# Expert features in order 8p+k: wider runs for the up weights, and rows turned by VectorE instead of TensorE

## The chip, the core and the metric

The kernel runs on one core of a Trainium2 chip. The metric is the device time of one execution in microseconds (us), as the median of several runs. The profiled execution is a separate one.

## What is computed

One layer of a hybrid backbone, for 512 sample tokens and 128 prompt tokens of 1024 features, all in fp32. A first part (modulated norm, one input projection, gated linear attention beside spatial gating, an output projection) is followed by a mixture of 16 experts in which each expert chooses its tokens. The second part, in which most of the time lies, is this:

```python
def ec_moe(x, router_w, w1, w3, w2):
    probs = jax.nn.softmax(jnp.matmul(xf, router_w), axis=-1)
    cap = EC_CAPACITY_FACTOR * N // N_EXPERTS            # 64 sample rows, 16 prompt rows
    gates, idx = lax.top_k(probs.T, cap)
    xe = xf[idx]
    h = jax.nn.silu(jnp.einsum('ecd,edf->ecf', xe, w1)) * jnp.einsum('ecd,edf->ecf', xe, w3)
    ye = jnp.einsum('ecf,efd->ecd', h, w2) * gates[..., None]
    out = jnp.zeros_like(xf).at[idx.reshape(-1)].add(ye.reshape(-1, D))
# in trunk_layer
    h2 = rmsnorm(x, norm2_w) * (1.0 + scale2) + shift2
    x = x + gate2 * ec_moe(h2, router_w, w1, w3, w2)
```

The weights w1 and w3 are 1024 x 2048 for each expert and w2 is 2048 x 1024: 24 MB an expert, 403 MB in all.

## The kernel before

Every engine runs its own list of instructions, written by hand, and semaphores join them. SyncE issues the loads of weights, ScalarE does activations and copies, VectorE the elementwise work and the 32x32 block transposes, GpSimd the loads and saves that are looked up by a table, TensorE the products and the turns of 128x128 tiles.

**Ahead of the experts.** The modulation vectors (shift, scale, gate, twice) come out of TensorE as rows in 12 pieces of 512 (`ada_product`), ScalarE copies them to `ada_rows`, TensorE turns them (`ada_turn`, L651 to L654, four turns each) and VectorE stores them in `mod` with the bias added (`store_mod`, L1391, L1393). Pieces 6 to 9 are shift 2 and scale 2, those of the mixture's norm. Feature f lies on partition f mod 128, in column f div 128 (order 128k+p). The normed rows `xn2` are turned by `route_turn` (L890), 8 tiles of 128 columns for each token tile, and multiplied with the router's weights. GpSimd saves each tile of `xn2` to DRAM (L585). VectorE finds the top tokens; the tables of slots are turned by TensorE (`all_slots`, L995).

**An expert.** TensorE holds 96 slots of rows (64 sample, 16 prompt, 16 empty) in three parts of 32 as `xe`, turned to [128 partitions, 8 kt, slots], and streams the weights past them (`up`, L1016, four products side by side in the array's four column groups). Weights come in 12 chunks of 2 MB an expert: 8 up chunks, w1 and w3 in turns, of two kt each, and 4 down chunks. They go through a ring of six slots; SyncE issues the next load of a slot when TensorE has read it (`load_expert_chunk`, L522). An up chunk is read by rows k*128+p, so that each partition's part is two runs of 8 KB; a down chunk is read by rows 16p+f, one run of 16 KB for each partition and 64 KB from partition to partition. The last up chunks of w1 and of w3 are done part by part, so that ScalarE (`silu`, L1321) and VectorE can start on part 0: the product with the gate (L1745) and the transpose of 32x32 blocks to `h` (L1749), which counts up `h_turned[part]`. The down products (`down_sample` L1032, `down_prompt` L1043) wait for `h_turned[0]` and `[1]`, and from the first `down_prompt` on for `[2]`.

**The next expert's rows.** GpSimd gathers 80 rows of 4 KB from the saved `xn2` to `xe_rows` (L588), TensorE turns them in eight tiles after the up products (`turn_xe`, L967), and VectorE multiplies by `amp2` and adds `mod`'s shift on the way to `xe` (`modulate`, L1662, L1667). GpSimd issues the gather for the expert after that when the turns are done. At the end of an expert VectorE scales the results (L1763, L1768, L1776) and GpSimd adds them to the rows in DRAM (scatter-add, L615). TensorE waits at the end of an expert for `xe` to be complete:

```python
                if not last:
                    pe.wait_ge(gathered, 32 + expert * 16)
                    for half in range(2):
                        wait_role_free(pe, f"X_{half}", expert)
                        role_filled(turn_xe(role_bank(f"X_{half}"), half), f"X_{half}")
                wait_role_free(pe, "Y_A", expert)
                wait_role_free(pe, "Y_B", expert)
                for part in range(PARTS - 1):
                    pe.wait_ge(h_turned[part], expert + 1)
```

## Time and profile before

| | us |
|---|---|
| median of 3 runs | 1450.53 (1450.44 to 1455.31) |
| the profiled execution | 1455.17 |
| its span | 1453.3 |
| TensorE busy (products) | 1391.0, 96% |
| VectorE busy | 356.9, 25% |
| ScalarE busy | 163.7, 11% |
| GpSimd busy | 56.0, 4% |
| bytes moved | 469.56 MB, mean 323 GB/s |

PE is TensorE's products, PEld its weight loads, DVE is VectorE, ACT ScalarE, POOL GpSimd, SPq SyncE's sequencer. L12 is line 12 of the kernel. Queue q1 is SyncE's, q10 ScalarE's and q0 GpSimd's. An fp32 product shows as two instructions, a turn as one. A row of the timeline or of the chain merges like instructions that follow one another. In the page's second part each digit or number is one of 40 equal slices of the span, here 36.3 us each.

### The profile page before, as it was taken

What the parts mean: (1) busy time and instruction counts of PE and PEld (TensorE: products, weight loads), DVE (VectorE), ACT (ScalarE), POOL (GpSimd) and SP (SyncE); (2) the same over time, 40 slices, a digit from 0 to 9 for tenths busy, and PEclk for the clock granted to TensorE, in tenths of its full rate; (3) what the DMA queues carried; (4) which work ended last, traced back from release to release, by engine and by line L of the source; (5) the groups of instructions that cost most, each with busy time, mean ns of one, the idle gap of its engine ahead of it and who ended that gap; (6) DMA issues with size and microseconds to landing.
All of it is one profiled execution on the core that took longest, in us unless ns stands there. A gap on an engine that the chain in (4) does not pass through costs nothing.

```text
span 1453.3 us, 24452 instructions
## 1 busy us (share of the span) xinstructions
PE 1391.0 (96%) x10960; PEld 511.1 (35%) x10960; DVE 356.9 (25%) x709; ACT 163.7 (11%) x263; POOL 56.0 (4%) x65
## 2 busy tenths in 40 slices
PE   5899999899879999999999999999999999999994
PEld 2354544755533232323333333332323333232321
DVE  3116153523632111303111130211203111130314
ACT  3263324111120000000000000000000000000011
POOL 0200000000000000000000000000000000000000
PEclk8999999799989999999999999999999999999997
DMA  9433313401656999999999999999999999999995
GB/s 358 160 118 115 107 51 109 154 30 58 263 222 279 396 409 413 411 417 400 426 402 412 414 412 417 401 412 414 410 417 402 425 399 412 414 410 417 414 411 213
DMA packets 73357, 469.56 MB, mean 323 GB/s; under 512 B 4749, under 2 KB 6626, under 8 KB 32362
## 3 DMA queue, kind: packets, MB, share of 16 engines
q1 hardware_dynamic: 67200, 451.36, 76.3%
q0 software_dynamic: 5200, 17.17, 4.2%
q10 hardware_dynamic: 922, 0.52, 0.1%
q8 instruction: 27, 0.44, 0.1%
q14 instruction: 8, 0.07, 0.0%
HBM read 455.67 MB, written 13.37 MB: 323 GB/s over the span
## 4 chain that ended last, share of the span: by engine, by line
PE 85%; DMA 11%; DVE 2%; issue 1%; SPq 1%; ACT 1%; POOLq 0%; ACTq 0%; POOL 0%; DVEq 0%
PE psum L1016 41%; PE psum L1032 12%; PE psum L663 9%; DMA ring<-in_exp_w_dram 9%; PE psum L1043 6%; PE psum L876 5%; PE psum L707 2%; PE psum L644 1%; DMA ring<-in_ada_w_dram 1%; PE psum L967 1%; PE psum L901 1%; PE psum L850 1%; SPq L546 1%; PE psum L854 1%; DMA both<-xn_dram,both 1%
## 5 line engine op out<-in xcount | busy, mean ns | idle before, releaser
L1016 PE MATMUL psum<-ring,both 128*32 128x512 f32 x6144 | 665.4, 593 | 1.9 <-DMA ring<-in_exp_w_dram 0.8
L1016 PEld LDWEIGHTS psum<-ring,both 128*32 128x32 f32 x6144 | 198.0, 110 | 462.7 <-issue 434.7
L1032 PE MATMUL psum<-ring,both 128*32 128x512 f32 x2048 | 233.6, 597 | 6.3 <-DMA ring<-in_exp_w_dram 5.8
L1745 DVE TENSOR_TENSOR both<-both,psum 128x512 f32<-128x512 f32 x48 | 49.5, 1032 | 555.4 <-PE psum L1016 555.4
L663 PE MATMUL psum<-ring,feat 128*128 128x512 f32 x320 | 138.3, 593 | 0.0
L1321 ACT ACTIVATE both<-psum 128x512 f32<-128x512 f32 x48 | 28.7, 597 | 952.1 <-PE psum L1016 887.1
L1032 PEld LDWEIGHTS psum<-ring,both 128*32 128x32 f32 x2048 | 65.2, 110 | 154.0 <-issue 143.8
L1043 PE MATMUL psum<-ring,both 128*32 128x512 f32 x1024 | 118.7, 592 | 0.0
L663 PEld LDWEIGHTS psum<-ring,feat 128*128 128x128 f32 x320 | 60.5, 190 | 76.4 <-issue 76.3
L1763 DVE SCALAR_TENSOR_TENSOR both<-psum,both 64x512 f32<-64x512 f32 x32 | 24.0, 749 | 224.2 <-PE psum L1043 224.0
L876 PE MATMUL psum<-ring,both 128*128 128x512 f32 x160 | 73.9, 618 | 0.0
L1043 PEld LDWEIGHTS psum<-ring,both 128*32 128x32 f32 x1024 | 33.4, 110 | 76.5 <-issue 75.9
L876 PEld LDWEIGHTS psum<-ring,both 128*128 128x128 f32 x160 | 31.1, 200 | 36.5 <-issue 36.4
L707 PE MATMUL psum<-feat,ring 128*128 128x512 f32 x64 | 32.0, 656 | 4.0 <-ACT feat L1152 2.4
L615 POOL DMA_INDIRECT acc_dram<-both x15 | 21.6, 1441 | 355.6 <-DVE both L1776 355.6
L588 POOL DMA_INDIRECT both<-xn_dram,both x15 | 13.8, 917 | 541.9 <-PE psum L967 541.6
L1749 DVE STREAM_TRANSPOSE both<-both 128x512 f32<-128x512 f32 x48 | 34.1, 711 | 1.7
L644 PE MATMUL psum<-ring,silu_c 128*32 128x512 f32 x192 | 26.3, 675 | 3.7 <-DMA ring<-in_ada_w_dram 3.1
L1776 DVE SCALAR_TENSOR_TENSOR both<-psum,both 64x512 f32<-64x512 f32 x32 | 24.0, 750 | 6.8 <-PE psum L1032 6.6
L1768 DVE TENSOR_TENSOR both<-both 32x512 f32<-32x512 f32 x32 | 21.9, 683 | 0.8
L1483 DVE SCALAR_TENSOR_TENSOR both<-both,chunk_decay 64x128 f32<-64x128 f32 x64 | 18.3, 347 | 14.7 <-ACT both L1225 14.3
L707 PEld LDWEIGHTS psum<-feat,ring 128*128 128x128 f32 x64 | 12.9, 208 | 21.2 <-issue 21.2
(221 smaller groups left out, 604.6 us busy)
## 6 DMA issues: line engine op xcount, KB each, us to landing
ring<-in_exp_w_dram SPq DMA_DIRECT2D x192, 2048.0 KB, 25.0
ring<-in_ada_w_dram SPq DMA_DIRECT2D x12, 2048.0 KB, 12.5
ring<-in_w_in_dram SPq DMA_DIRECT2D x4, 2048.0 KB, 12.8
ring<-in_w_out_dram SPq DMA_DIRECT2D x2, 2048.0 KB, 10.6
acc_dram<-x POOLq DMA_DIRECT2D x5, 512.0 KB, 2.9
xn_dram<-feat POOLq DMA_DIRECT2D x5, 512.0 KB, 2.9
x<-acc_dram SPq DMA_DIRECT2D x5, 512.0 KB, 26.5
out_dram<-feat SPq DMA_DIRECT2D x5, 512.0 KB, 10.4
```

The source lines that it names most:

```text
L644: mm = nc.tensor.matmul(bank(n)[gr * PART:(gr + 1) * PART, :], silu_c[:, kt, :], w[:, kt, :], start=(i == 0), stop=(i == 1))
L663: mm = nc.tensor.matmul(bank(n), hT[:, kt, t * P:(t + 1) * P], w[:, kt, :], start=(kt == 0), stop=(kt == KT - 1))
L707: return nc.tensor.matmul(bank(JOB["qkS", m]), w[:, kt, m * P:(m + 1) * P], hT[:, kt, 0:SAMPLE], start=(kt == 0), stop=(kt == KT - 1))
L876: mm = nc.tensor.matmul(bank(n), mixT[:, t % 2, kt, :], w[:, kt, :], start=(kt == 0), stop=(kt == KT - 1))
L1016: mm = nc.tensor.matmul(role_bank(role)[f4 * PART:(f4 + 1) * PART, :], xe[:, kt, part * PART:(part + 1) * PART], w[:, kt % 2, f4 * 512:(f4 ...
L1032: mm = nc.tensor.matmul(role_bank("Y_A")[at:at + PART, :], h[:, c, part * PART:(part + 1) * PART], w[:, f, half * 512:(half + 1) * 512], s ...
L1043: mm = nc.tensor.matmul(role_bank("Y_B")[at:at + PART, :], h[:, c, 2 * PART:PADDED], w[:, f + odd, half * 512:(half + 1) * 512], start=(c ...
L1321: role_stored(nc.scalar.activation(silu_h[:, r % 2, :], role_bank(role), ACT.Silu), role)
L1745: role_stored(nc.vector.tensor_tensor(h_rows[:, part, :].rearrange("p (c a) -> p a c", a=PART), silu_h[:, part % 2, :].rearrange("p (a c) ...
L1749: nc.vector.transpose(h[:, :, part * PART:(part + 1) * PART], h_rows[:, part, :].rearrange("p (c a) -> p c a", a=PART))\
L1763: ins = nc.vector.scalar_tensor_tensor(y_pair[:, odd, :], y_b[rows], prob_now[rows, 1:2], gate2_p[rows], ALU.mult, ALU.mult)
L1776: ins = nc.vector.scalar_tensor_tensor(y[0:CAP_S, cols], y_a[rows], prob_now[rows, 0:1], gate2_s[rows], ALU.mult, ALU.mult)
```

## The change

The features of the mixture's input are held in order 8p+k (feature 8p+k on partition p, column k) instead of 128k+p. For this:

- an up chunk is read by rows 8p+k, two neighbouring rows at a time: one run of 16 KB for each partition, 64 KB from partition to partition; the router's weights are read in the same order;
- norm2's weights and the biases of shift 2 and scale 2 are loaded in this order by three small DMAs of GpSimd (`vecs2`); pieces 6 to 9 of the modulation are turned by `ada_turn_by_row`, eight products of 64 stepped columns of `ada_rows` against `sel` (128 x 2, which sums the row groups), and stored by `store_mod_by_row`;
- `route_turn` and the turns of the first expert's rows take every eighth column (`by_row`);
- a gather fetches each row in four quarters of 1 KB, quarter a of slot s to partition 32a+s, in three DMAs of 128 quarters (`xq`), with three more tables of indices (`slot_quarter`), worked out by five small VectorE operations and turned by three more of TensorE;
- VectorE transposes the 32x32 blocks of `xq` straight to `xe` (three instructions of 128x256) and applies amplitude and shift in four operations on whole slot ranges; this stands where `modulate` stood, after the transposes of `h`;
- TensorE's eight turns per expert, its waits for them and their PSUM roles go; TensorE waits for `xe_ready` at the head of experts 1 to 15; GpSimd issues the three gathers for the expert after next when VectorE has turned `xq`.

```diff
@@ load_expert_chunk
-                    src = (w1, w3)[which][0, bass.ds(expert, 1)].rearrange("a (k p) n -> p (a k) n", p=P)[:, 2 * k2:2 * k2 + 2, :]
+                    src = (w1, w3)[which][0, bass.ds(expert, 1)].rearrange("a (p k) n -> p (a k) n", p=P)[:, 2 * k2:2 * k2 + 2, :]
@@ gpsimd
-            pool.dma_start(router, router_w[0].rearrange("(k p) e -> p k e", p=P)).then_inc(router_loaded, 16)
+            pool.dma_start(router, router_w[0].rearrange("(p k) e -> p k e", k=KT)).then_inc(router_loaded, 16)
+            for i, src in enumerate((norm2_w[0], ada_b[0, 128 * SHIFT2:128 * SHIFT2 + D], ada_b[0, 128 * SCALE2:128 * SCALE2 + D])):
+                pool.dma_start(vecs2[:, i, :], src.rearrange("(p k) -> p k", k=KT)).then_inc(vecs2_loaded, 16)
             def gather(expert):
-                pool.indirect_dma_start(out=xe_rows, out_offset=None, in_=xn2_dram,
-                                        in_offset=bass.IndirectOffsetOnAxis(ap=slot_tok[0:SLOTS, expert:expert + 1], axis=0))\
-                    .then_inc(gathered, 16)
+                for part in range(PARTS):
+                    pool.indirect_dma_start(out=xq[:, part, :], out_offset=None, in_=xn2_dram.rearrange("t (a n) -> (t a) n", a=4),
+                                            in_offset=bass.IndirectOffsetOnAxis(ap=slot_quarter[:, part, expert:expert + 1], axis=0))\
+                        .then_inc(gathered, 16)
...
-                    wait_role_filled(pool, "X_0", expert)
-                    wait_role_filled(pool, "X_1", expert)
+                    pool.wait_ge(xq_turned, expert + 1)
                     gather(expert + 2)
@@ tensor
+            def ada_turn_by_row(c5):
+                wait_stored(pe, JOB["adaR", c5])
+                pe.wait_ge(sel_ready, 1)
+                n = JOB["adaT", c5]
+                wait_bank_free(pe, n)
+                rows = ada_rows[:, ADA_ORDER.index(c5) % 2, :].rearrange("p (m k) -> p k m", k=KT)
+                at = (c5 % 2) * (P // 2)
+                for k8 in range(KT):
+                    mm = nc.tensor.matmul(bank(n)[at:at + P // 2, 2 * k8:2 * k8 + 2], rows[:, k8, :], sel, start=True, stop=True)
+                filled(mm, n)
...
+            def by_row(rows):
+                return rows.rearrange("p (m k) -> p k m", k=KT)
...
-                        mm = nc.tensor.transpose(bank(n)[:, j * P:(j + 1) * P], xn2[:, t, kt * P:(kt + 1) * P], ident)
+                        mm = nc.tensor.transpose(bank(n)[:, j * P:(j + 1) * P], by_row(xn2[:, t, :])[:, kt, :], ident)
...
-                for i in range(5):
+                for i in range(8):
                     mm = nc.tensor.transpose(bank(n)[:, i * EXPERTS:(i + 1) * EXPERTS], top_rows[:, i, :], ident[0:EXPERTS, 0:EXPERTS])
...
+                if not first:
+                    pe.wait_ge(xe_ready, expert)
...
-                if not last:
-                    pe.wait_ge(gathered, 32 + expert * 16)
-                    for half in range(2):
-                        wait_role_free(pe, f"X_{half}", expert)
-                        role_filled(turn_xe(role_bank(f"X_{half}"), half), f"X_{half}")
...
-                if not last:
-                    for half in range(2):
-                        wait_role_stored(pe, f"X_{half}", expert)
@@ vector, expert_work
-                    for half in range(2):
-                        wait_role_filled(dve, f"X_{half}", expert)
-                        role_stored(modulate(role_bank(f"X_{half}"), half, link_expert), f"X_{half}")
+                    dve.wait_ge(gathered, 16 + 48 + expert * 48)
+                    for part in range(PARTS):
+                        ins = nc.vector.transpose(xe[:, :, part * PART:(part + 1) * PART], xq[:, part, :].rearrange("p (i k) -> p k i", k=KT))
+                    ins.then_inc(xq_turned, 1)
+                    dve.wait_ge(xq_turned, expert + 1)
+                    kinds = ((slice(0, CAP_S), 0), (slice(CAP_S, PADDED), 1))
+                    for slots, w in kinds:
+                        shape = [P, KT, slots.stop - slots.start]
+                        ins = nc.vector.tensor_tensor(xe[:, :, slots], xe[:, :, slots], amp2[:, :, w:w + 1].to_broadcast(shape), ALU.mult)
+                    link_expert(ins)
+                    for slots, w in kinds:
+                        shape = [P, KT, slots.stop - slots.start]
+                        ins = nc.vector.tensor_tensor(xe[:, :, slots], xe[:, :, slots], mod[:, SHIFT2:SHIFT2 + KT, w:w + 1].to_broadcast(shape),
+                                                      ALU.add)
+                    ins.then_inc(xe_ready, 1)
```

## Rows read from the trace of the kernel before

**Rows 1.** The page: engine TensorE, and the rate of the 40 slices.

```profile
PE 1391.0 (96%) x10960; PEld 511.1 (35%) x10960; DVE 356.9 (25%) x709; ACT 163.7 (11%) x263; POOL 56.0 (4%) x65
...
GB/s 358 160 118 115 107 51 109 154 30 58 263 222 279 396 409 413 411 417 400 426 402 412 414 412 417 401 412 414 410 417 402 425 399 412 414 410 417 414 411 213
```

**Rows 2.** Busy time in 14 periods, one for each of experts 1 to 14.

```profile
core 0: us, PE busy (x) PEld busy (x) DVE busy (x) ACT busy (x) POOL busy (x), PEclk, DMA share, GB/s
489.80:552.90 63.10, 62.76 (x588) 19.05 (x584) 11.60 (x22) 1.79 (x3) 2.42 (x2) 1.00 1.01 409
...
678.80:741.40 62.60, 62.60 (x588) 19.21 (x584) 11.63 (x21) 1.79 (x3) 2.35 (x2) 1.00 1.01 412
...
sum 879.30, PE 878.38 PEld 268.07 DVE 162.69 ACT 25.08 POOL 32.11; mean PE 62.74 PEld 19.15 DVE 11.62 ACT 1.79 POOL 2.29
```

**Rows 3.** The chain that ended last, 660 to 760 us: start, us, what.

```profile
678.76 41.20 PE psum L1016 x384
719.96 0.70 PE psum L967 x8
720.67 3.57 PE psum L1032 x32
```

**Rows 4.** SyncE's loads L522 issued in 741 to 804 us: issue to landing.

```profile
DMA to landing us min/median/max: 23.7/24.8/25.1
```

**Rows 5.** DMA queues (packets, MB, share) in 714-724, 736-746 and 752-762 us.

```profile
q1 hardware_dynamic: 293, 4.28, 100.4%
...
q1 hardware_dynamic: 545, 4.20, 100.9%
...
q1 hardware_dynamic: 554, 4.28, 101.1%
```

**Rows 6.** DMA queues in 726-731 us (a gather) and 748-752 us (a scatter-add).

```profile
q1 hardware_dynamic: 97, 1.39, 84.5%
q0 software_dynamic: 82, 0.29, 17.4%
...
q1 hardware_dynamic: 138, 1.06, 64.3%
q0 software_dynamic: 94, 0.32, 40.1%
```

**Rows 7.** DMA queues in 44-47 us (512 B beside 2 KB) and 26-29 us.

```profile
q1 hardware_dynamic: 427, 0.87, 80.3%
q10 hardware_dynamic: 426, 0.22, 25.8%
...
q1 hardware_dynamic: 569, 1.16, 105.0%
```

**Rows 8.** Timeline, DVE 714 to 745 us, then PE 700 to 860 us.

```profile
718.40 1.01 DVE L1745 TENSOR_TENSOR both<-both,psum 128x512 f32<-128x512 f32 x1
719.44 0.71 DVE L1749 STREAM_TRANSPOSE both<-both 128x512 f32<-128x512 f32 x1
...
721.13 0.71 DVE L1749 STREAM_TRANSPOSE both<-both 128x512 f32<-128x512 f32 x1
...
738.11 1.51 DVE L1763 SCALAR_TENSOR_TENSOR both<-psum,both 64x512 f32<-64x512 f32 x2 [14.17 <-PE psum L1043]
...
719.90 0.77 PE L967 MATMUL psum<-consts,both 80*128 80x80 f32 x8
720.60 3.64 PE L1032 MATMUL psum<-ring,both 128*32 128x512 f32 x32
```

**Rows 9.** Timeline of PE and DVE ahead of the experts' loop.

```profile
212.85 0.60 PE L653 MATMUL psum<-consts,both 128*128 128x128 f32 x4
...
424.32 1.96 PE L901 MATMUL psum<-router_amp,both 128*128 128x16 f32 x16
...
408.24 0.67 DVE L1557 TENSOR_TENSOR both<-psum,both 128x512 f32<-128x512 f32 x1
...
417.95 0.42 DVE L1662 TENSOR_TENSOR both<-psum,amp 128x256 f32<-128x256 f32 x1 [1.31 <-PE psum L976]
```

## What is predicted, and why

> **What bounds the kernel now.** I read the page first: TensorE is busy for 96% of the span, and from slice 14 on the core moves 396 to 426 GB/s in every slice [rows 1]. So the page leaves two candidates for the sixteen experts, which fill everything behind 420 us. The table by expert then gives the period. From the first up product of expert 1 (489.8 us) to that of expert 15 (1369.1 us) pass 879.3 us, 62.80 us for each of 14 experts, with the DMA share at 1.01 and the clock at full in each of them [rows 2]. The first period is 63.10 us, the fourth 62.60.
>
> TensorE's own part of a period comes from the chain: 41.20 us of up products, 0.70 us of turns of the next expert's rows, 3.57 us for the first group of down products [rows 3], and five more groups of 3.43 us worth of products; eight up chunks and four down chunks are 12 times 5.15 = 61.8 us, and with the turns 62.5 us. The queue's own part comes from the issues: in the period from 741 us on a 2 MB load lands 23.7 to 25.1 us after its issue [rows 4]. At the 5.0 us that one load takes (next paragraph), that is five loads waiting or moving, out of six slots, so the queue is nearly never empty. Both servers thus need 62.5 to 62.8 us, and whichever edit helps only one of them is worth little. That is the main thing to see.
>
> **Up weights in 16 KB runs.** I priced them from stretches in which only SyncE's queue moved. The semaphore writes (32 in 10 us) are taken off the count. Of the down weights, which already come in 16 KB runs with 64 KB from run to run, 261 packets took 100.4% of 16 engines for 10 us: 160.6/261 = 0.615 us each. Of the up weights' 8 KB packets there are two levels: 513 packets at 100.9% make 0.315 us, 522 at 101.1% make 0.310 us; mean 0.3125 [rows 5]. A chunk costs each engine 16 x 0.3125 = 5.00 us now and 8 x 0.615 = 4.92 us then. The new up pattern (16 KB runs, 64 KB apart) is just that of the down weights, so I take their price. Saved: 0.08 us a chunk (0.04 to 0.12 by the two levels), 0.64 us an expert. The queue's period goes from 62.80 to 62.16 us if the gather costs what it did.
>
> **The gather as quarters.** Today 80 packets of 4 KB are fetched while 16 KB packets run. In 726 to 731 us 1.68 MB moved, which at the 428 GB/s of the neighbouring stretch takes 3.93 us; 1.07 us are lost beside the 0.77 us of the gather's own 0.33 MB: 1.84 us a gather, 0.37 us for each of an engine's 5 packets [rows 6]. The scatter-add, same count at 748 to 752 us, costs about 1.5 us in the same way, and stays [rows 6]. The new gather moves 384 packets of 1 KB, 24 an engine. No 1 KB packets beside a busy queue are in the trace. The nearest rows are the 512 B packets beside 2 KB ones at 44 to 47 us: 418 of them take 25.8% of 3 us, 0.030 us each, while the 2 KB packets beside them stay at 0.090 us, against 0.089 us with nothing beside them [rows 7]. By a line through 512 B (0.030) and 2 KB (0.089) a 1 KB packet is 0.05 us, 24 of them 1.2 us: 0.6 us less than now. The other end is the present price per packet, 24 x 0.37 = 8.8 us: 7 us more. In between, the present price by bytes: 1.84 x 0.393/0.328 = 2.2 us, 0.4 us more. I take the middle of the first and the third, 1.7 us, because the packets nearest in size slow nobody and the packets nearest in path (same queue, same table) slow others; that is about no change. The queue's period is then 62.1 us (61.5 to 62.6, and up to 69 in the rival below).
>
> **No turns on TensorE.** The eight turns go, 0.70 us each time, 15 times: 10.5 us of TensorE's time. But they cover something. The first down product waits for h of parts 0 and 1. VectorE finishes the product of part 1 at 719.41 and its transpose at 720.15; TensorE's up products end at 719.9, so the turns up to 720.60 hide that wait [rows 8]. With them gone TensorE stands still from 719.9 to about 720.2. The saving is 720.6 - 720.2 = 0.4 us an expert, not 0.7. h of part 2 is there at 721.84 and needed 3.4 us into the down products: no wait. TensorE's period becomes 62.5 - 0.4 = 62.1 us.
>
> **What VectorE takes over.** Behind the last h transpose (721.84) come three transposes of 128x256 and four elementwise operations. The transpose of 128x512 takes 0.71 us [rows 8], so 0.36 us each. An operation that writes at a step (the h product, 1.01 us) is 1.5 times one of the same shape that doesn't (0.67 us) [rows 8, 9], so with the stepped reads up to 0.55 us each. Elementwise: two of 512 columns (0.7) and two of 256 (0.42). In all 3.3 to 3.9 us, done by 725.8. VectorE's next job starts at 738.11 [rows 8], and TensorE's new wait for xe comes at 741: hidden with 12 us to spare. If a gather landed more than 40 us late this wait would show; it has a whole period. Queued behind VectorE's new wait for the gather are the y products, needed from 738 on. GpSimd's three gathers per expert are issued at about 723; even at one 1 KB packet for each 16 KB packet they are through after 24 x 0.665 = 16 us, ahead of the scatter-add, which is queued behind them and starts at about 743.
>
> **Ahead of the experts.** Turns of shift and scale 6 to 9 become eight matmuls against two columns. Four turn instructions take 0.60 us; small matmuls run in pairs of passes, 16 in 1.96 us, 0.12 us each [rows 9], so 16 instructions cost up to 2.0 us, or 1.3 if two columns are a third cheaper. Turns 6 and 7 stand on TensorE's chain: +0.7 to +1.4 us each. Turns 8 and 9 come before TensorE waits for VectorE: nothing. Reads at a 32 B step in the token turns, three more small transposes, three tiny loads on GpSimd's queue, five small VectorE operations more for the slot table: covered by waits of TensorE for VectorE or DMA, 0 to +2 us. I take +2 in all (0 to +5).
>
> **The sum.** The larger of 62.1 and 62.1 us, with a little for two servers that are equal (today 62.80 against 62.5 and 62.8): 62.3 us. 14 x (62.80 - 62.3) = 7.0 us, and for the turns of expert 0 and the up chunks of expert 15 0.8 us. Less 2 us ahead: 5.8 us. The profiled execution took 1455.2 us (span 1453.3) and would take 1449.4; it stands 4.6 us above the median of the runs, 1450.5. Against the median: **1444.7 us**, own range 1442 to 1449. A measurement of this kernel can tell about 0.5% (7.25 us) from no change, so faster means under 1443.3, slower over 1457.8.
>
> **Rivals.**
> A. *The gather becomes cheap and the start costs nothing.* For it: the 512 B packets of [rows 7]. Against it: equal servers never reach their floor. Period 62.2, 14 x 0.6 + 0.8 = 9.2 us, less 0 to 1: 1441.8. Chance 0.27. The swizzle rule above would lead here.
> B. *The gather takes back what the runs give.* It costs 2.5 us, 0.7 more than now; period 62.8, only the start moves: 1449 to 1453. Chance 0.15. An up weight's 16 KB run that is no faster than its two halves ends here as well.
> C. *Small packets are paid by the piece (slower).* Place: the queue, 727 to 745 us of each period. Above 0.105 us a packet (24 x 0.105 = 2.5 us) the gather eats the gain; at half of today's price per piece, 0.185 us, it costs 4.4 us, 2.6 more than now, period 64.8, 14 x 2.0 + 2 = 30 us: 1480. For it: 4 KB gather packets cost 0.37 us where 0.154 us would be their bytes. Chance 0.12.
> D. *The start costs more,* because weights are loaded at a 32 B step in some 60 turns: 0.1 to 0.2 us each, 6 to 12 us, with the gain of the experts at half: 1450 to 1459. Chance 0.08, half of it over 1457.8. The Trainium skill, "SBUF — State Buffer", section "Door 1: The DMA port swizzle", says that reads which leave a 16-byte line each time pay a penalty; the trace agrees for VectorE's writes (1.01 against 0.67 us) and shows nothing of TensorE.
>
> The forecast has 0.38. **Chances:** faster 0.27 + 0.08 of the forecast's range = 0.35; slower 0.12 + 0.04 and 0.02 for a stall not thought of = 0.18; same 0.47. The range takes in A, the forecast, B and D: 1439.5 to 1460.
>
> **What would show it.** Right: SyncE's packets of 16 KB at 0.615 us throughout; a period of 62.3 us; the first down product 0.3 us behind the last up product, released by VectorE's transpose; the next expert's xe ready at 726. Wrong: 16 KB packets of the up weights above 0.63 us; a gather stretch of more than 2.5 us lost; TensorE waiting at the head of an expert for VectorE; a first up product of expert 1 that is late by more than the 2 us.

## The result, and the profile after

The changed kernel takes 1439.53 us (median of 5 runs, 1436.43 to 1440.22), the kernel before 1450.44 us (5 runs, 1448.50 to 1455.31): a ratio of 0.992, 95% interval 0.990 to 0.994, 10.9 us faster. The forecast was 5.8 us faster. Later runs of the changed kernel on another chip gave 1442.38 us beside 1451.82 us for the kernel before, 9.4 us faster.

The page of the profiled execution (its time 1439.8 us). The lines answer to [rows 1]; behind them are the page's lines on queues and issues.

```profile
span 1438.0 us, 24229 instructions
PE 1378.7 (96%) x10891; PEld 565.4 (39%) x10891; DVE 383.0 (27%) x704; ACT 163.1 (11%) x263; POOL 93.3 (6%) x98
GB/s 357 162 125 101 98 49 111 183 30 59 245 245 259 416 426 419 427 421 416 430 417 427 420 427 421 417 430 416 426 422 426 419 416 430 418 427 419 404 406 123
q0 software_dynamic: 6016, 18.17, 4.2%
ring<-in_exp_w_dram SPq DMA_DIRECT2D x192, 2048.0 KB, 17.4
x<-acc_dram SPq DMA_DIRECT2D x5, 512.0 KB, 14.8
```

A weight load now lands 17.4 us after its issue in the median; before it was 25.0. A load is issued when its slot of the ring has been read, and its chunk is needed five chunks later, by my estimate after 5 x 5.15 = 25.8 us. What is left between landing and need I call the queue's lead: before it was under 2 us in the loop's middle, and in the changed kernel it grows from expert to expert. The landing of the loads issued in 1300 to 1355 us (least, median, most), first before, then changed:

```profile
DMA to landing us min/median/max: 21.9/23.7/24.9
```

```profile
DMA to landing us min/median/max: 8.9/10.2/11.3
```

Earlier in the changed kernel the median was 23.1 us (issued in 560 to 620 us) and 20.0 us (741 to 804 us, against the 24.8 of [rows 4]). Next the stretches: 14 periods (from the first up product of expert 1 to that of expert 15), and the last expert up to the first of the two save instructions that GpSimd issues last. First the changed kernel, then the kernel before, whose 14 periods are those of [rows 2] to within 0.3 us.

```profile
core 0: us, PE busy (x) PEld busy (x) DVE busy (x) ACT busy (x) POOL busy (x), PEclk, DMA share, GB/s
485.20:1357.80 872.60, 868.05 (x8068) 315.46 (x8064) 186.34 (x280) 25.07 (x42) 63.85 (x53) 1.00 1.01 422
1357.80:1428.30 70.50, 62.25 (x580) 22.39 (x572) 21.94 (x29) 10.96 (x21) 2.41 (x3) 0.98 0.77 308
```

```profile
489.30:1368.90 879.60, 878.68 (x8184) 268.16 (x8180) 162.93 (x294) 25.08 (x42) 32.11 (x27) 1.00 1.01 412
1368.90:1446.20 77.30, 64.28 (x580) 18.90 (x572) 21.90 (x29) 11.43 (x21) 2.36 (x2) 0.95 0.86 348
```

The periods are 872.6/14 = 62.33 us each, with no scatter beyond 0.01 us: 7.0 us less in all. The last expert takes 70.5 instead of 77.3 us: 6.9 us less. Where those went shows in the waits of TensorE (engine, line, waited for: us in total, times, longest) in the last expert of the kernel before:

```profile
PE psum L1032 <- DMA ring<-in_exp_w_dram: 4.6, 1, 4.6
PE psum L1032 <- DVE both L1749: 0.5, 1, 0.5
```

In the changed kernel only the second kind is left there. Behind the wait of 4.6 us TensorE also works at a lower clock. The first row is its group of down products behind the wait, which takes 5.34 us where the same group takes 3.65 us in the changed kernel; the other two are 1421.2 to 1423 and 1423 to 1425 us, with a granted clock of 0.58 and 0.52, so mostly at the lower of the two levels (1.2 GHz of 2.4):

```profile
1421.21 5.34 PE L1032 MATMUL psum<-ring,both 128*32 128x512 f32 x32 [4.64 <-DMA ring<-in_exp_w_dram]
1421.20:1423.00 1.80, 1.79 (x12) 0.59 (x16) 1.80 (x3) 0.00 (x0) 0.00 (x0) 0.58 1.03 437
1423.00:1425.00 2.00, 2.00 (x12) 0.44 (x8) 2.00 (x2) 0.00 (x0) 0.00 (x0) 0.52 1.00 426
```

So the 6.9 us are some 4.8 us of waiting, 1.7 us of slower products behind it, and 0.4 us up to the first down product, of which 0.2 us are a wait for weights. The chain of one period of the changed kernel answers to [rows 3]:

```profile
672.38 41.20 PE psum L1035 x384
713.58 0.33 issue
713.90 3.64 PE psum L1051 x32
717.54 1.72 PE psum L1062 x16
719.26 3.43 PE psum L1051 x32
```

The 0.70 us of turns are gone, a pause of 0.33 us stands in their place, and the first group of down products takes 3.64 instead of 3.57 us. VectorE's timeline of the same place (to be held against [rows 8]) gives the cause of the pause: the second h transpose ends at 713.80 (713.09 + 0.71), and the down products start at 713.90.

```profile
713.09 0.71 DVE L1795 STREAM_TRANSPOSE both<-both 128x512 f32<-128x512 f32 x1
713.73 1.03 DVE L1791 TENSOR_TENSOR both<-both,psum 128x512 f32<-128x512 f32 x1
714.79 0.71 DVE L1795 STREAM_TRANSPOSE both<-both 128x512 f32<-128x512 f32 x1
715.42 1.67 DVE L1802 STREAM_TRANSPOSE both<-both 128x256 f32<-128x256 f32 x3
717.12 1.03 DVE L1808 TENSOR_TENSOR both<-both,amp 128x512 f32<-128x512 f32 x2
718.18 1.03 DVE L1812 TENSOR_TENSOR both<-both,mod 128x512 f32<-128x512 f32 x2
731.41 1.51 DVE L1821 SCALAR_TENSOR_TENSOR both<-psum,both 64x512 f32<-64x512 f32 x2 [12.19 <-PE psum L1062]
```

### The profile page after: what moved, and what is told of

Same layout as the page of the kernel before. It is cut to its first block, busy times and chain, and to the rows that moved or that the text cites. A ratio compares the mean times of both kernels' runs of the same rounds, so it can differ in the third digit from the quotient of the medians.

```text
span 1438.0 us, 24229 instructions
## 1 busy us (share of the span) xinstructions
PE 1378.7 (96%) x10891; PEld 565.4 (39%) x10891; DVE 383.0 (27%) x704; ACT 163.1 (11%) x263; POOL 93.3 (6%) x98
## 4 chain that ended last, share of the span: by engine, by line
PE 93%; DVE 3%; DMA 2%; issue 1%; ACT 1%; POOLq 0%; ACTq 0%; POOL 0%; DVEq 0%
PE psum L1035 45%; PE psum L1051 15%; PE psum L685 10%; PE psum L1062 8%; PE psum L898 5%; PE psum L729 2%; PE psum L654 1%; DMA both<-xn_dram,both 1%; PE psum L927 1%; DMA ring<-in_ada_w_dram 1%; PE psum L872 1%; PE psum L876 1%; PE psum L760 0%; PE psum L699 0%; DMA ring<-in_pos_col_dram 0%
## 5 line engine op out<-in xcount | busy, mean ns | idle before, releaser
L1035 PEld LDWEIGHTS psum<-ring,both 128*32 128x32 f32 x6144 | 238.7, 110 | 419.4 <-issue 416.1
L685 PE MATMUL psum<-ring,feat 128*128 128x512 f32 x320 | 138.3, 593 | 0.0
L1051 PEld LDWEIGHTS psum<-ring,both 128*32 128x32 f32 x2048 | 78.5, 110 | 150.1 <-issue 150.1
L685 PEld LDWEIGHTS psum<-ring,feat 128*128 128x128 f32 x320 | 60.5, 190 | 76.4 <-issue 76.3
L600 POOL DMA_INDIRECT both<-xn_dram,both x45 | 49.4, 1099 | 578.5 <-DVE both L1802 569.1
L1062 PEld LDWEIGHTS psum<-ring,both 128*32 128x32 f32 x1024 | 40.3, 110 | 69.6 <-issue 69.3
L625 POOL DMA_INDIRECT acc_dram<-both x15 | 22.1, 1471 | 274.7 <-DVE both L1834 274.7
L1802 DVE STREAM_TRANSPOSE both<-both 128x256 f32<-128x256 f32 x45 | 25.1, 609 | 0.0
## 6 DMA issues: line engine op xcount, KB each, us to landing
ring<-in_exp_w_dram SPq DMA_DIRECT2D x192, 2048.0 KB, 17.4
```

Source lines behind the costliest of these rows:

```text
L600: pool.indirect_dma_start(out=xq[:, part, :], out_offset=None, in_=xn2_dram.rearrange("t (a n) -> (t a) n", a=4), in_offset=bass.IndirectO ...
L685: mm = nc.tensor.matmul(bank(n), hT[:, kt, t * P:(t + 1) * P], w[:, kt, :], start=(kt == 0), stop=(kt == KT - 1))
L1035: mm = nc.tensor.matmul(role_bank(role)[f4 * PART:(f4 + 1) * PART, :], xe[:, kt, part * PART:(part + 1) * PART], w[:, kt % 2, f4 * 512:(f4 ...
L1051: mm = nc.tensor.matmul(role_bank("Y_A")[at:at + PART, :], h[:, c, part * PART:(part + 1) * PART], w[:, f, half * 512:(half + 1) * 512], s ...
L1062: mm = nc.tensor.matmul(role_bank("Y_B")[at:at + PART, :], h[:, c, 2 * PART:PADDED], w[:, f + odd, half * 512:(half + 1) * 512], start=(c ...
L1802: ins = nc.vector.transpose(xe[:, :, part * PART:(part + 1) * PART], xq[:, part, :].rearrange("p (i k) -> p k i", k=KT))
```

## The experiments

In the table the start is where the first up product of expert 1 begins, the loop the mean of 14 periods, the last expert runs from its first up product to the first of the last two saves, and the end from there to the end of the span. They are read from the timelines of TensorE and GpSimd in each kernel's one profiled execution. The median is that of the runs.

| kernel | start | period | last expert | end | median us |
|---|---|---|---|---|---|
| before | 489.3 | 62.83 | 77.4 | 7.0 | 1450.44 |
| before again | 483.3 | 62.89 | 77.7 | 7.0 | 1449.48 |
| changed | 485.2 | 62.33 | 70.4 | 9.7 | 1439.53 |
| changed again | 486.4 | 62.33 | 70.4 | 9.7 | 1442.38 |
| before, 16 KB runs | 485.8 | 62.64 | 70.4 | 7.0 | 1440.32 |
| changed, 8 KB runs | 482.0 | 62.37 | 70.5 | 9.7 | 1440.61 |
| changed, row gather | 487.4 | 62.41 | 73.0 | 7.3 | 1444.96 |
| changed, 8 KB runs and row gather | 488.6 | 62.85 | 77.5 | 7.3 | 1452.49 |
| changed, turns back | 487.2 | 62.64 | 70.4 | 9.7 | 1444.85 |
| before, small reload | 489.1 | 62.85 | 70.8 | 7.0 | 1444.91 |
| changed, part 2 last | 482.5 | 61.80 | 69.7 | 9.7 | 1433.73 |
| changed, part 2 last, again | 487.6 | 61.80 | 69.7 | 9.7 | 1433.74 |
| changed, old turns at the start | 481.7 | 62.33 | 70.4 | 9.7 | 1441.98 |
| before, filler | 488.6 | 62.76 | 77.9 | 7.1 | 1454.46 |

The times of single runs of one kernel scatter by some us either way. The periods and the last expert's time scatter far less: two executions of the changed kernel agree to 0.01 us in the period and 0.1 us in the last expert, two of the kernel before to 0.06 and 0.3 us. So the verdicts rest on these two columns.

**Runs alone.** The kernel before, with the up chunks read by rows 8p+k; the products pair other features, the work is the same.

```diff
-                    src = (w1, w3)[which][0, bass.ds(expert, 1)].rearrange("a (k p) n -> p (a k) n", p=P)[:, 2 * k2:2 * k2 + 2, :]
+                    src = (w1, w3)[which][0, bass.ds(expert, 1)].rearrange("a (p k) n -> p (a k) n", p=P)[:, 2 * k2:2 * k2 + 2, :]
```

> The kernel before with one edit: up chunks are read by rows 8p+k, so in 16 KB runs, while xe keeps its old order (the products mix other features; the work is the same). Theory 1, two equal servers: the queue loses 0.6 us of work an expert, TensorE's 62.5 us stay; the period falls from 62.80 to 62.6 us, 3 us over the loop, and as the queue gains a small lead, part of the 5.8 us that TensorE waits for it at the end of expert 15 goes: 1444 to 1448 us in all, 2 to 6 us less than before. Theory 2, TensorE was the bound all along and the turns are the whole gain: nothing, 1449 to 1451 us. Theory 3, the queue was the bound: 62.2 us and 8 us or more less, 1442 us or below.

Measured: 1440.32 us (4 runs, 1438.73 to 1442.05), beside 1451.87 us for the kernel before on the same chip, ratio 0.993 (0.990 to 0.995). Its two stretches:

```profile
485.80:1362.80 877.00, 877.00 (x8184) 269.11 (x8180) 162.81 (x294) 25.09 (x42) 32.10 (x27) 1.00 1.01 416
1362.80:1433.10 70.30, 62.16 (x580) 19.63 (x572) 21.90 (x29) 10.87 (x21) 2.36 (x2) 0.97 0.86 348
```

The period is 62.64 us, which is TensorE's floor with turns: in these 14 periods it is never idle, and a load lands after 22.1 us in the median instead of 25.0 (18.8 us in 1300 to 1355 us). The loop gives 2.6 us, as theory 1 has it, but the last expert gives the whole 7 us, more than theory 1 had. The total is that of theory 3, whose period of 62.2 us did not come. This one edit reaches the time of the whole change.

**The changed kernel without the runs.** The same line the other way round.

> The changed kernel with up chunks read by rows 128k+p again, in 8 KB runs (the products mix other features). Theory 1: the queue then needs 8 x 5.00 + 4 x 4.92 = 59.7 us for the weights, 1.0 for the cheap gather and 1.7 for the scatter-add, 62.4 us against TensorE's 62.33: period 62.4 to 62.5, landing back from 17 to about 25 us, and part of the wait at the end returns; 1441 to 1445 us against 1439.5. Theory 2: no difference, 1439 to 1440.

Measured: 1440.61 us (4 runs, 1437.23 to 1442.44), ratio 0.994 (0.991 to 0.996). Period 62.84 us once, then 62.33; last expert 70.5 us. Theory 2 holds: the period is TensorE's, not the 62.4 to 62.5 us of theory 1, and no wait comes back at the end. With the cheap gather the queue stays below TensorE's 62.33 us even in 8 KB runs. What it loses is lead: landing 21.7 instead of 17.4 us in the median (17.9 against 10.2 us in 1300 to 1355 us).

**The changed kernel with the old gather.** Experts 1 to 15 then work on rows that the gather doesn't fill.

```diff
             def gather(expert):
-                for part in range(PARTS):
-                    pool.indirect_dma_start(out=xq[:, part, :], out_offset=None, in_=xn2_dram.rearrange("t (a n) -> (t a) n", a=4),
-                                            in_offset=bass.IndirectOffsetOnAxis(ap=slot_quarter[:, part, expert:expert + 1], axis=0))\
-                        .then_inc(gathered, 16)
+                pool.indirect_dma_start(out=xe_rows, out_offset=None, in_=xn2_dram,
+                                        in_offset=bass.IndirectOffsetOnAxis(ap=slot_tok[0:SLOTS, expert:expert + 1], axis=0))\
+                    .then_inc(gathered, 16)
...
-                    dve.wait_ge(gathered, 16 + 48 + expert * 48)
+                    dve.wait_ge(gathered, 16 + 16 + expert * 16)
```

> The changed kernel with the old gather: one DMA of 80 rows of 4 KB to 80 partitions instead of three of 128 quarters; VectorE transposes the same amount, from memory that the gather doesn't fill (the experts 1 to 15 work on other numbers). Theory 1 (the gather to 128 partitions became cheap, 1.0 us of the queue instead of 1.8): the queue needs 59.1 + 1.8 + 1.7 = 62.6 us, period 62.6 against 62.33, 4 us over the loop and 2 to 4 us at the end: 1443 to 1448 us. Theory 2: no difference, 1439 to 1440. In the trace the 16 KB packets beside the gather go from 0.636 back to about 0.83 us under theory 1.

Measured: 1444.96 us (10 runs, 1436.05 to 1451.07), ratio 0.996 (0.993 to 0.998). Against theory 1 the period stays at 62.33 us after the first; the last expert takes 73.0 us, 2.6 more than in the changed kernel, with a wait of 2.4 us for weights. So the median lies in theory 1's range, but not for its reason: the 59.1 + 1.8 + 1.7 = 62.6 us that I added up for the queue are some 0.3 us too much. The gather's own price is close to the expected one: (5 - 1.73 MB/429) + 0.32/429 = 1.7 us, and 0.77 instead of 0.83 us for a 16 KB packet beside it. The queues while a gather runs (packets, MB, share of 16 engines), first this kernel in 725 to 730 us, then the changed kernel in 722 to 728 us:

```profile
DMA packets 195, 1.73 MB, mean 347 GB/s; under 512 B 30, under 2 KB 30, under 8 KB 109
q1 hardware_dynamic: 101, 1.41, 82.8%
q0 software_dynamic: 94, 0.32, 19.2%
```

```profile
DMA packets 290, 2.55 MB, mean 425 GB/s; under 512 B 66, under 2 KB 66, under 8 KB 157
q1 hardware_dynamic: 151, 2.18, 88.0%
```

The row gather pulls the rate down to 347 GB/s, as in [rows 6]. Beside the quarters it is 425 GB/s, against 429 in an undisturbed stretch (736 to 741 us). So a gather of quarters costs its bytes, 0.393 MB/429 = 0.92 us, and next to nothing more: 2.55 MB/429 is 5.94 of the 6 us. The two gathers differ in the size of their pieces, in the number of their DMAs and in the number of partitions; no run tells these apart.

**Both helps to the queue taken away.** The two edits above together; what is left of the change is TensorE without turns, and the start.

> The changed kernel with both helps to the queue taken away: up chunks in 8 KB runs and the old gather of 80 rows (the products mix other features, and VectorE transposes memory that the gather doesn't fill). What is left of the change is TensorE without turns, and the start. Theory 1 (equal servers): TensorE's floor is 62.33 us but the queue needs as long as before, so the period stays at 62.7 to 62.8 us and the last expert, from its first up product to the last save, takes 77 us as before instead of 70.4: 1448 to 1451 us, nearly the whole gain gone. Theory 2 (the turns are the gain): 62.33 and 70.4 us, 1440 us.

Measured: 1452.49 us (10 runs, 1445.91 to 1455.59), ratio 1.000 (0.998 to 1.002). Its two stretches:

```profile
488.60:1368.40 879.80, 870.94 (x8068) 285.32 (x8064) 186.16 (x280) 25.10 (x42) 36.44 (x27) 1.00 1.01 412
1368.40:1446.00 77.60, 64.29 (x580) 19.80 (x572) 21.90 (x29) 11.52 (x21) 2.41 (x3) 0.95 0.86 349
```

They are the stretches of the kernel before, to 0.3 us. Taking the turns from TensorE is worth nothing by itself: over the 14 periods it is busy for 7.7 us less and idle for 8.0 us more (8.9 against 0.9 us). Of these 8.9 us the pauses for h are at most 14 x 0.33 = 4.6 us, the rest is waiting for weights. Its weight loads show the same: 53.2 us in 93 waits for the queue, against 35.9 us in 62 before.

**Turns back on TensorE.** The changed kernel with eight turns of a constant behind the up products.

```diff
+                if not last:
+                    wait_role_stored(pe, "R1_0", expert)
+                    for j in range(8):
+                        nc.tensor.transpose(role_bank("R1_0")[:, (j % 4) * SLOTS:(j % 4 + 1) * SLOTS], ident[0:SLOTS, :], ident[0:SLOTS, 0:SLOTS])
                 wait_role_free(pe, "Y_A", expert)
```

> The changed kernel with eight turns of 80x128 on TensorE put back behind the up products (they turn a constant; nobody reads them). If the turns cover the wait for h, as the prediction said: the 0.33 us of waiting go and 0.70 us of turns come, period 62.33 + 0.4 = 62.7 us, 15 x 0.4 = 6 us more, 1445 to 1446 us. If the wait were not covered by them, 15 x 0.7 = 10.5 us more, 1450 us.

Measured: 1444.85 us (10 runs, 1440.20 to 1449.06), ratio 0.995 (0.993 to 0.997). All 14 periods are 62.64 us: 0.31 us more than 62.33, 14 x 0.31 = 4.3 us; the last expert, which has no turns, is level (70.4 us). The turns did cover the wait for h; without them TensorE gets 0.31 us, not 0.70 (and not the 0.4 of the prediction).

**The reload in the last expert.** The kernel before, with 64 of 1024 columns of x reloaded; the final norm of the other columns works on old values.

```diff
-                        sp.dma_start(x[:, t, :], acc_dram[t * P:(t + 1) * P, :]).then_inc(acc_loaded[t], 16)
+                        sp.dma_start(x[:, t, 0:64], acc_dram[t * P:(t + 1) * P, 0:64]).then_inc(acc_loaded[t], 16)
```

> The kernel before, but of the 2.6 MB of x that are reloaded during the last expert only 64 of 1024 columns are (0.16 MB; the final norm works on old values for the rest). Theory L1: the 7 us that the last expert took longer before (77.4 to 77.9 against 70.4 us from its first up product to the last save) are the reload, which a queue without a lead can't hide: the last expert falls to 71 to 72 us, the loop stays at 62.8 us a period, 1444 to 1445 us. Theory L2: they come from the lag that the queue has gathered over the loop: 77 us still, 1450 us.

Measured: 1444.91 us (10 runs, 1441.59 to 1448.91), ratio 0.995 (0.993 to 0.997). The two stretches:

```profile
489.10:1369.00 879.90, 878.77 (x8182) 268.12 (x8178) 162.93 (x294) 25.07 (x42) 32.10 (x27) 1.00 1.01 412
1369.00:1439.80 70.80, 62.38 (x580) 19.65 (x572) 21.91 (x29) 11.05 (x21) 2.38 (x3) 0.97 0.86 346
```

L1 holds: same loop, and the last expert is 70.8 us. It is the bytes and not the issuing: SyncE stands 9.15 us at the five reloads in this kernel, and 9.14 us in the kernel before, and here no wait follows. The 2.6 MB of x that SyncE loads ahead of the last three chunks of w2 are 6.1 us of the queue at 429 GB/s. How much of them reaches TensorE goes with the lead at the end of the loop:

| kernel | landing of loads issued in 1300 to 1355 us, median | wait for weights behind the reload | last expert |
|---|---|---|---|
| before | 23.7 | 4.6 | 77.4 |
| changed, row gather | 20.7 | 2.4 | 73.0 |
| before, 16 KB runs | 18.8 | 0.3 | 70.4 |
| changed | 10.2 | none | 70.4 |

A queue that is 3 us further ahead than before halves the wait, one that is 5 us further ahead hides nearly all of it.

**The start.** Three kernels. First the changed one with pieces 6 to 9 of the modulation turned and stored the old way, which leaves amplitude and shift of the mixture out of order:

```diff
-            ada_turn_by_row(6)
+            ada_turn(6)
...
-            store_mod_by_row(6, 7)
+            store_mod(6, 7)
```

(and so for pieces 7, 8 and 9).

> The changed kernel with pieces 6 to 9 of the modulation turned and stored the old way (four turns each, vectors in order 128k+p, so amplitude and shift of the mixture are out of order). TensorE saves 2.01 - 0.44 = 1.6 us at each of turns 6 and 7, 3.1 us on its chain. Theory S1, the start was priced right: 3 us less, 1436 to 1437 us. Theory S2, the small products of turns 8 and 9 fill a gap and keep TensorE's clock high afterwards (clock 0.79 before, 0.94 after in 254 to 290 us): without them the clock falls for about 10 us more and 3 us or so come back: 1439 to 1441 us, with the granted clock at 0.8 in the stretch of the first attention tiles.

Then the kernel before again, and the kernel before with 32 small products of constants in TensorE's gap behind piece 9.

> The kernel before again, for a second profile. Its first profiled execution took 1455.2 us and stood 4.7 above the median. If that excess lies ahead of the experts (a longer stretch at half clock), the first up product of expert 1 comes 3 to 4 us earlier than 489.8 us in an execution of 1450 us, and the loop is the same 62.8 us a period. If it lies in the loop, the start is the same and the periods are 62.5.

```diff
             ada_turn(8)
             ada_turn(9)
+            wait_bank_free(pe, JOB["attF", 0])
+            for i in range(32):
+                nc.tensor.matmul(bank(JOB["attF", 0])[0:64, 0:2], ident[:, 0:64], ident[:, 0:2], start=True, stop=True)
```

> The kernel before with 32 small products of constants (64 columns against 2, two passes each, nobody reads them) behind the turns of pieces 8 and 9, where TensorE waits 5.4 us for VectorE. Theory S2 (filling the gap keeps the clock): the granted clock in 254 to 290 us rises from 0.79 to 0.9 or more and the kernel is 2 to 4 us faster, 1446 to 1448 us. Theory S1: no difference, 1450 us.

Measured: old turns 1441.98 us (6 runs, 1436.31 to 1443.11), before again 1449.48 us (10 runs, 1442.66 to 1454.27), filler 1454.46 us (10 runs, 1443.35 to 1460.56; ratio 1.000, 0.997 to 1.003). The old turns show no gain in the median, against 1439.53 and 1442.38 us of the changed kernel, so neither theory's total can be told from the scatter. The kernel before had its first up product of expert 1 at 483.3 us this time, 6.0 us earlier, and the same period (62.89 us): its first excess lay ahead of the experts. From the first projection (L663, L685 in the changed kernel) to the first mixing product (L813, L835) TensorE takes 155.90 us in each kernel with the old turns and 159.05 us in each with the new ones: the new turns of pieces 6 and 7 cost 3.15 us, 2.01 us each where 0.44 us stood. One of them in the chain of the changed kernel (start, length, engine, line):

```profile
213.45 2.01 PE psum L675 x16
```

and the four in its instructions by line (least, median and most ns of one):

```profile
L675 PE MATMUL psum<-sel,both x64: 259/259/282, 213.4 to 265.3; 128*64 128x2 f32 x64
```

A later stretch, from the first attention output product (L850, L872) to the first product of the router's bias (L912, L938), varies between executions of the same kernel: 18.8 and 18.6 us in two executions of the kernel before, 14.5 and 18.4 us in two of the changed one. Theory S2 falls twice: the filler leaves the clock as it was, and the kernel with the old turns has a granted clock of 0.91 in 254 to 290 us where S2 had 0.8. The stretch 254 to 290 us of the filler kernel, then of the changed kernel:

```profile
254.00:290.00 36.00, 35.14 (x296) 31.02 (x295) 20.43 (x50) 5.15 (x11) 0.00 (x0) 0.78 0.42 154
```

```profile
254.00:290.00 36.00, 34.20 (x291) 27.74 (x284) 21.61 (x56) 6.05 (x13) 0.00 (x0) 0.94 0.48 179
```

TensorE is busy for 35.1 us in the first and still granted 0.78. What sets the length of the low stretches wasn't found. With it the start as a whole (483.3 to 489.3 us in executions of the kernel before, 485.2 and 486.4 in two of the changed one) can't be told apart, nor over all the kernels of the table: 485.9 us is the mean of the eight with the new turns, 486.3 us of the six with the old ones. Only the 3.15 us are sure.

**The changed kernel again,** for its second profile:

> The changed kernel again, beside the others on one chip, for a second profile: period 62.33 us, last expert 70.4 us; the stretch from the first projection to the first mixing product 159.05 us (155.90 before). If the stretch behind it (to the first product of the router's bias) is 14.5 us again, the change makes it shorter; if it is 16.5 to 18.8 us as in other runs, its length comes from where the clock's low stretches fall.

1442.38 us (6 runs, 1439.99 to 1445.80), ratio 0.994 (0.992 to 0.997). Periods 62.33 us, last expert 70.4 us, and 159.05 us again; the later stretch took 18.4 us, so its length is not the change's.

**Part 2 last.** The pause of 0.33 us can be filled: of the last up chunks parts 0 and 1 are done first, so that h of part 1 has 3.4 us of products behind it.

```diff
-                for which in range(2):
-                    w = up_chunk(which, KT // 2 - 1)
-                    for part in range(PARTS):
-                        for kt in (KT - 2, KT - 1):
-                            up(which, part, kt, w)
+                for parts in ((0, 1), (2,)):
+                    for which in range(2):
+                        w = up_chunk(which, KT // 2 - 1)
+                        for part in parts:
+                            for kt in (KT - 2, KT - 1):
+                                up(which, part, kt, w)
```

> The changed kernel with one edit: of the last up chunks of w1 and w3, parts 0 and 1 are done first (w1 then w3), then part 2 (w1 then w3). The product of part 1 is then complete 3.4 us before the end of the up products instead of 1.7 us, so h of part 1 (2.1 us behind it) is ready when TensorE comes to the down products, and h of part 2 is ready 2.1 us after the end, needed at 3.4 us. The wait of 0.33 us at each expert goes: period 62.33 to 62.0 us, 16 x 0.33 = 5.2 us less, 1434 to 1435 us, if the queue (59.1 + 1.0 + 1.7 = 61.8 us) keeps up. Rival, the queue becomes the bound at 62.2: 2 to 3 us less, 1437 us.

> The version with part 2 of the last up chunks last, again and on the same chip as the changed kernel: period 61.8 us against 62.33, 14 x 0.53 = 7.4 us in the loop and 0.7 us in the last expert; 6 to 8 us less than the changed kernel, about 1432 us.

Measured: 1433.73 us (6 runs, 1428.93 to 1437.69; ratio to the kernel before 0.988, 0.985 to 0.990), and 1433.74 us (6 runs, 1432.57 to 1437.95; 0.989, 0.986 to 0.991), where the changed kernel stood at 1442.38. Two groups of the chain (second execution):

```profile
639.72 12.88 PE psum L1035 x120
652.60 3.43 PE psum L1051 x32
```

The period is 61.80 us, just the sum of 12 chunks of 5.15 us. I had expected 62.0: the wait cost not only its pause (0.33 us) but also 0.21 us in the first group behind it (3.64 against 3.43 us). The rival falls too: the queue needs no more than 61.8 us. This version beats both kernels.

## Why the prediction was wrong

The direction was right, the size was about half (5.8 against 10.9 us). The step that failed is the term for the ends of the loop, 0.8 us where 6.9 us were measured in the last expert alone. Step by step:

- *Equal servers.* Right for the loop: runs alone take it to TensorE's floor and no further (62.64), turns alone leave it with the queue (62.85). Wrong for the total: "whichever edit helps only one of them is worth little" does not hold for the runs, which alone bring the time of the whole change. The forecast period of 62.3 us was 62.33, and the loop's 7.0 us were 7.0. That it hit so well is partly luck. TensorE's floor was 62.64 us and not 62.5: the first group of down products, which follows the turns without a pause, takes 3.57 and not 3.43 us, and the prediction's own rows add up to 62.62. The turns gave 0.31 us and not 0.4. TensorE's period was thus 62.33 and not 62.1, and the 0.2 us added for two equal servers, which were no longer equal, made up for it. The queue's period came out below 62.1: it holds 61.80 with part 2 last. From the growth of its lead (landing 23.1 us at about 590 us, 10.2 us at about 1328 us, 11.8 periods later) I estimate 62.33 - 1.09 = 61.2 us. The same estimate gives 62.2 us for runs alone (23.9 to 18.8 us), which is the 62.16 of the prediction.
- *The turns cover the wait for h.* Right, shown by putting turns back: TensorE waits 0.33 us where I wrote 0.3.
- *The gather.* I took 1.7 us in a range from 1.2 to 8.8. It is 0.9 to 1.0, just below the cheap end, which is why the queue came out lower. The quarters don't show as 1 KB packets: 15 expert gathers would be 5760 of them, and q0 grew by 816 packets only, from 5200 to 6016. In place of 1440 packets that carried rows or semaphore counts (15 x 96) it has 2160 (15 x 144), and 96 come from the three small loads: an expert then has 96 data packets of 4 KB, four quarters each, and 48 counts, and the core's packets of 2 to 8 KB did grow by 240, 15 x 16. That price by the piece was the ground of rival C, and it falls; rival A was right on the gather. The rule on the swizzle from the Trainium skill ("DMA: Bandwidth & Descriptors", "The descriptor swizzle") fits the two gathers: beside the one to 128 partitions the core moves 425 GB/s, beside the one to 80 it moves 347. Which engine wrote which partition no trace here shows, so that the swizzle is the reason stays open.
- *The last expert.* This is the step that failed. I gave it, with the turns of expert 0, 0.8 us; it was 6.9 us. I priced each server's mean period and let the sum end there. But the same queue also carries the reload of x (2.6 MB) in the last expert, and the prediction has no term for it, though TensorE's wait of 4.6 us stands in the profile of before, and a slower clock behind the wait adds 1.7 us. The small reload shows the cause, and runs alone shows that a lead of some 5 us more is enough to hide it. So a lead in the queue that is worth nothing in the loop is worth 7 us at its end.
- *The start.* I took +2 us. The sure part is +3.15 us, 1.57 for each turn and above the 0.7 to 1.4 us of the prediction; what hides it in the totals wasn't resolved. The stepped reads of the token turns cost next to nothing on the chain: a weight load of them takes 0.19 instead of 0.14 us, but eight turns stand there with 0.88 to 0.90 us as before with 0.87 to 0.88. That was the ground of rival D.
- *The end.* Not in the sum: from the first of the last two saves to the end of the span it takes 9.7 instead of 7.0 us.

The account is 7.0 + 6.9 - 2.7 = 11.2 us if the start is level, and 8.1 us if its sure 3.15 us count in full; the medians gave 10.9 and, in the repetition, 9.4. The two first profiled executions differ by 15.3 us: the start of the kernel before was 4.1 us later, within its own scatter.

VectorE's part held: the new work ended at 719.2 us in the period shown, 12 us ahead of its next job. The stepped transposes cost 0.61 us each (45 of them), a little above my bound of 0.55; the whole new work took 3.8 us, inside the 3.3 to 3.9.

## What to carry to other kernels

Where two servers need the same time, price the edit of each against the other's floor: either alone may give a fraction, and the order in which they are made decides which of them seems to have paid (here 8 KB runs cost nothing once the gather was cheap, and the runs alone gave everything while it was not). Then follow the faster queue to its end: what it carries besides the loop (here a reload in the last round) is hidden by its lead, so look at the waits of the first and the last round, not of the middle only. And when an instruction block is removed that stood between a producer and its reader, look for what can be put in its place; reordering three lines gave the rest.

## What the runs showed of the hardware that was not expected

- An indirect gather of 1 KB pieces to 128 partitions moves in packets of 4 KB and costs its bytes (425 of 429 GB/s beside it); one of 4 KB rows to 80 partitions pulls the core's rate to 347 GB/s.
- The same group of down products takes 3.43 us when it follows the up products directly, 3.57 us behind the eight turns, without a pause, and 3.64 us behind a pause of 0.33 us. Behind a wait of 4.6 us it took 5.34 us, at a granted clock of 0.52 to 0.58 over its first 3.8 us.
- Sixteen products of 64 columns against 2, fp32, take 2.01 us (0.126 us each), as long as sixteen of 128 columns against 16 (1.96 us, [rows 9]).
- The stretch between the first of the last two saves and the end of the span is 9.7 us in every kernel with the gathers of quarters and 7.0 to 7.3 us in every one without. The page lists 98 GpSimd instructions in the changed kernel against 65 before. That the number of its indirect DMAs sets it is only a guess.
